# Latent attention in groups of two blocks, with four score banks and one output bank

## What is computed

```python
def mixer_mla(u, w_in, q_norm, w_uq, kv_norm, w_ukv, w_out):
    cq, ckv, k_rope, gate = jnp.split(u @ w_in, [...], axis=-1)
    q = (rmsnorm(cq, q_norm) @ w_uq).reshape(B, S, 16, 64 + 32)
    kv = (rmsnorm(ckv, kv_norm) @ w_ukv).reshape(B, S, 16, 64 + 64)
    ...
    s = (einsum('bqhd,bkhd->bhqk', q_nope, k_nope) + einsum('bqhd,bkd->bhqk', q_rope, k_rope)) * scale
    p = softmax(s, axis=-1)
    o = einsum('bhqk,bkhd->bqhd', p, v)
    return (o * silu(gate)) @ w_out
```

## Time and profile before

| | |
|---|---|
| median of 3 runs | 2837.42 us (2836.51 to 2840.32) |
| profiled execution, its own time | 2842.69 us |
| its span, mean granted clock | 2840.9 us, 0.995 |
| TensorE matmuls busy in the span | 2789.1 us (98%) |
| TensorE weight loads busy | 2323.7 us (82%) |
| VectorE, ScalarE, GpSimd busy | 1366.9, 940.3, 1237.5 us |

### The profile page before, as it was taken

One profiled execution on the slowest core, in us unless ns is written; L12 is line 12 of the kernel. 1 busy time (PEld: TensorE's weight loads), 2 busy tenths in 40 slices (PEclk: granted clock), 3 DMA queues, 4 the chain that ended last, 5 costly groups with the idle time before them and its releaser, 6 DMA issues.

```text
span 2840.9 us, 36776 instructions
## 1 busy us (share of the span) xinstructions
PE 2789.1 (98%) x13634; PEld 2323.7 (82%) x13634; DVE 1366.9 (48%) x1892; ACT 940.3 (33%) x1316; POOL 1237.5 (44%) x913
## 2 busy tenths in 40 slices
PE   7999999999999999999999999999999999999998
PEld 5888887887888888888888878888888888888886
DVE  4544566658646443046443066646442075554412
ACT  3333434763224222243222243433222231322222
POOL 2453235113554454424545533234545545354554
PEclk9999999999999999999999999999999999999999
DMA  7664234102333333332333322122333333233332
GB/s 270 181 193 129 82 94 123 36 24 67 105 95 90 96 96 96 108 105 82 96 96 104 104 83 79 59 75 89 96 96 104 104 89 97 67 114 94 100 100 95
DMA packets 106123, 284.97 MB, mean 100 GB/s; under 512 B 38669, under 2 KB 38797, under 8 KB 104675
## 3 DMA queue, kind: packets, MB, share of 16 engines
q1 hardware_dynamic: 99360, 257.64, 30.4%
q10 hardware_dynamic: 6643, 25.64, 2.7%
HBM read 280.98 MB, written 8.85 MB: 102 GB/s over the span
## 4 chain that ended last, share of the span: by engine, by line
issue 42%; PE 33%; POOL 24%; DVE 1%; DMA 0%; POOLq 0%; ACT 0%; SPq 0%
POOL w_lo L624 24%; PE ps L435 11%; PE ps L437 11%; PE ps L436 11%; DMA w_raw<-in_stream 0%; DVE x L2326 0%; DVE tmp L2320 0%; PE ps L485 0%; POOLq L622 0%; POOLq L166 0%; PE ps L513 0%; PE ps L496 0%; PE ps L480 0%; DVE u_lo L2126 0%; ACT u_hi L1557 0%
## 5 line engine op out<-in xcount | busy, mean ns | idle before, releaser
L624 POOL TENSOR_TENSOR w_lo<-w_raw,w_hi 128x512 fp32r<-128x512 f32 x904 | 1236.6, 1391 | 1590.0 <-ACT w_hi L428 1590.0
L435 PE MATMUL ps<-u_hi,w_hi 128*128 128x512 f32 x2296 | 905.3, 394 | 9.2 <-DVE u_lo L2126 5.4
L437 PE MATMUL ps<-u_hi,w_lo 128*128 128x512 f32 x2296 | 897.7, 391 | 0.0
L436 PE MATMUL ps<-u_lo,w_hi 128*128 128x512 f32 x2296 | 897.5, 391 | 0.0
L428 ACT ACTIVATE w_hi<-w_raw 128x1024 fp32r<-128x1024 f32 x452 | 475.7, 1055 | 799.2 <-PE ps L437 767.3
L435 PEld LDWEIGHTS ps<-u_hi,w_hi 128*128 128x128 f32 x2296 | 433.7, 189 | 105.6 <-DVE u_lo L2126 8.6
L437 PEld LDWEIGHTS ps<-u_hi,w_lo 128*128 128x128 f32 x2296 | 433.3, 189 | 91.2
L436 PEld LDWEIGHTS ps<-u_lo,w_hi 128*128 128x128 f32 x2296 | 433.5, 189 | 90.5 <-issue 1.9
L437 PE MATMUL ps<-h_hi,w_lo 128*128 128x512 f32 x704 | 273.9, 389 | 0.0
L435 PE MATMUL ps<-h_hi,w_hi 128*128 128x512 f32 x704 | 273.9, 389 | 0.0
L436 PE MATMUL ps<-h_lo,w_hi 128*128 128x512 f32 x704 | 273.9, 389 | 0.0
(11 more groups left out here) (307 smaller groups left out, 3089.4 us busy)
## 6 DMA issues: line engine op xcount, KB each, us to landing
w_raw<-in_stream SPq DMA_DIRECT2D x452, 512.0 KB, 3.6
late_ring<-in_ada_late ACTq DMA_DIRECT2D x32, 512.0 KB, 5.0
ada_ring<-in_ada SPq DMA_DIRECT2D x8, 1024.0 KB, 10.4
dilated_bias_rows<-dilated_bias SPq DMA_DIRECT2D x18, 244.1 KB, 5.2
band_a<-dilated_bias_rows SPq DMA_DIRECT2D x96, 28.0 KB, 2.0
x<-in_x SPq DMA_DIRECT2D x8, 256.0 KB, 8.1
bias_rows<-bias_scratch ACTq DMA_DIRECT2D x4, 512.0 KB, 7.8
out_yT<-x SPq DMA_DIRECT2D x8, 256.0 KB, 2.0
```

Source lines behind the costliest of these rows:

```text
L435: nc.tensor.matmul(o, w[0], v[0], start=start, stop=False)
L436: nc.tensor.matmul(o, w[0], v[1], start=False, stop=False)
L437: return nc.tensor.matmul(o, w[1], v[0], start=False, stop=stop)
L624: ins = nc.gpsimd.tensor_tensor(w_lo[:, s, half], w_raw[:, s, half], w_hi[:, s, half].bitcast(F32), ALU.subtract)
```

## The change

Two blocks form a group, on all three engines. TensorE issues both scores of the next group, then what there is for the next pairs, then both turns of this group, then a spread if one is due, then the values of the two blocks ahead of them. The first query product of the pair after next moves to the last group of a pair (that of pair 1 ahead of the loop), the keys to the first group and the second query product to the second group. Scores use four banks (3 to 6) in place of three (4 to 6), maxima four columns in place of two, outputs the one bank 2 in place of banks 2 and 3. TensorE now waits for all value copies before its first score, since bank 3 is one of theirs. ScalarE does both exponentials ahead of a group's two copies. VectorE does both maxima first, waits for a bank's exponential of four blocks ago in place of the last one, and takes the finished pair's steps in the four groups of the next pair; the low part of an output comes in the last group of the next pair, and at the end ahead of the last denominators.

```diff
--- before.py
+++ after.py
@@ -952,11 +952,11 @@
                 if b == 0:
                     pe.wait_ge(q_evac, Q0 + 2 * p + hh + 1)
                     pe.wait_ge(k_evac, K0 + p + 1)
-                if i >= 3:
-                    pe.wait_ge(s_read, R0 + i - 2)
+                if i >= 4:
+                    pe.wait_ge(s_read, R0 + i - 3)
                 q = [t[:, p % 2, hh, b * P:(b + 1) * P] for t in (qb_hi, qb_lo)]
                 k = [t[:, p % 2, hh, :] for t in (kb_hi, kb_lo)]
-                product(bank(4 + i % 3), q, k, True, True).then_inc(s_done, 1)
+                product(bank(3 + i % 4), q, k, True, True).then_inc(s_done, 1)
 
             def b_turn(i):
                 pe.wait_ge(s_read, R0 + i + 1)
@@ -969,12 +969,12 @@
             def b_pv(i):
                 p, b = i // 8, i % 8 // 2
                 pe.wait_ge(t_evac, T0 + i + 2)
-                if b == 0 and p >= 2:
-                    pe.wait_ge(o_evac, O0 + p - 1)
+                if b == 0 and p:
+                    pe.wait_ge(o_evac, O0 + p)
                 for k in range(QB):
                     for hh in range(2):
                         r = slice(64 * hh, 64 * hh + 64)
-                        mm = pe.matmul(ps[r, 2 + p % 2, b * P:(b + 1) * P],
+                        mm = pe.matmul(ps[r, 2, b * P:(b + 1) * P],
                                        vb[:, k, p * P + 64 * hh:p * P + 64 * hh + 64], ptb[:, (i + hh) % 3, k, :],
                                        start=k == 0, stop=k == QB - 1)
                 mm.then_inc(o_done, 2)
@@ -1005,25 +1005,28 @@
                 product(bank(j % 4), (ck_hi[:, b * P:(b + 1) * P], ck_lo[:, b * P:(b + 1) * P]),
                         (w_hi[:, slot, w], w_lo[:, slot, w]), True,
                         True).then_inc(v_turned if j < 2 * QB - 1 else chunk_used, 1)
+            pe.wait_ge(v_ready, V0 + 2 * QB)
             b_scores(0)
             b_scores(1)
-            pe.wait_ge(v_ready, V0 + 2 * QB)
-            for i in range(NB_BLOCKS):
-                p, step = i // 8, i % 8
+            b_queries(1, 0)
+            for i in range(0, NB_BLOCKS, 2):
+                p, step = i // 8, i % 8 // 2
                 if i + 2 < NB_BLOCKS:
                     b_scores(i + 2)
-                if p + 1 < NPAIR and step == 2:
-                    b_keys(p + 1)
-                b_turn(i)
-                if i and i % 2 == 0:
-                    b_pv(i - 2)
+                    b_scores(i + 3)
                 if p + 1 < NPAIR:
                     if step == 0:
-                        b_queries(p + 1, 0)
-                    if step == 4:
+                        b_keys(p + 1)
+                    elif step == 1:
                         b_queries(p + 1, 1)
-                if p and step == 6:
+                if p + 2 < NPAIR and step == 3:
+                    b_queries(p + 2, 0)
+                b_turn(i)
+                b_turn(i + 1)
+                if p and step == 2:
                     b_spread(p - 1)
+                if i:
+                    b_pv(i - 2)
             b_spread(NPAIR - 1)
             b_pv(NB_BLOCKS - 2)
 
@@ -1605,7 +1608,7 @@
                 if i >= 4:
                     act.wait_ge(t_done, T0 + i - 3)
                 at = QB * (i % 2) + i % 8 // 2
-                nc.scalar.activation(pb[:, i % 4, :], bank(4 + i % 3), ACT.Exp, bias=col[:, i % 2:i % 2 + 1],
+                nc.scalar.activation(pb[:, i % 4, :], bank(3 + i % 4), ACT.Exp, bias=col[:, i % 4:i % 4 + 1],
                                      accum_out=den[:, i // 8 % 3, at:at + 1]).then_inc(s_read, 1)
 
             chunk("b_first", 0)
@@ -1621,27 +1624,34 @@
                 nc.scalar.activation(vb[:, b, half * S:(half + 1) * S], bank(j % 4), ACT.Copy).then_inc(v_ready, 1)
             chunk("b_v", 0)
             b_exp(0)
-            for i in range(NB_BLOCKS):
-                p, step = i // 8, i % 8
-                if i + 1 < NB_BLOCKS:
-                    b_exp(i + 1)
+            b_exp(1)
+            b_query_hi(1, 0)
+
+            def b_turned(i):
                 act.wait_ge(t_done, T0 + i + 1)
                 if i >= 3:
                     act.wait_ge(o_done, T0 + 2 * ((i - 3) // 2) + 2)
                 nc.scalar.activation(ptb[:, i % 3, :, :].rearrange("p k e -> p (k e)"), bank(i % 2),
                                      ACT.Copy).then_inc(t_evac, 1)
+
+            for i in range(0, NB_BLOCKS, 2):
+                p, step = i // 8, i % 8 // 2
+                if i + 2 < NB_BLOCKS:
+                    b_exp(i + 2)
+                    b_exp(i + 3)
+                b_turned(i)
                 if p + 1 < NPAIR:
                     if step == 0:
-                        chunk("b_pair", p)
-                    if step == 1:
-                        b_query_hi(p + 1, 0)
-                    if step == 2:
                         b_keys(p + 1)
-                    if step == 5:
+                    elif step == 1:
                         b_query_hi(p + 1, 1)
-                if p >= 2 and step == 0:
-                    b_output_hi(p - 2)
-            b_output_hi(NPAIR - 2)
+                if p + 2 < NPAIR and step == 3:
+                    b_query_hi(p + 2, 0)
+                b_turned(i + 1)
+                if p + 1 < NPAIR and step == 0:
+                    chunk("b_pair", p)
+                if p and step == 3:
+                    b_output_hi(p - 1)
             b_output_hi(NPAIR - 1)
 
             norm_out(1, "b_out")
@@ -2230,7 +2240,7 @@
 
             def b_output(p):
                 dve.wait_ge(o_done, T0 + 8 * p + 8)
-                nc.vector.scalar_tensor_tensor(out=tmp[:, 2 + p % 2, :], in0=bank(2 + p % 2), scalar=0.5,
+                nc.vector.scalar_tensor_tensor(out=tmp[:, 2 + p % 2, :], in0=bank(2), scalar=0.5,
                                                in1=ggb[:, p, :], op0=ALU.mult, op1=ALU.mult).then_inc(o_evac, 1)
 
             def b_denominators(p):
@@ -2250,7 +2260,9 @@
 
             def b_max(i):
                 dve.wait_ge(s_done, R0 + i + 1)
-                nc.vector.tensor_reduce(col[:, i % 2:i % 2 + 1], bank(4 + i % 3), AX.X, ALU.max,
+                if i >= 4:
+                    dve.wait_ge(s_read, R0 + i - 3)
+                nc.vector.tensor_reduce(col[:, i % 4:i % 4 + 1], bank(3 + i % 4), AX.X, ALU.max,
                                         negate=True).then_inc(m_ready, 1)
 
             for hh in range(2):
@@ -2264,37 +2276,38 @@
                     b_key_lo(0, 0)
                     b_key_lo(0, 1)
             b_max(0)
-            for i in range(NB_BLOCKS):
-                p, step = i // 8, i % 8
+            b_max(1)
+            dve.wait_ge(grp_done, GRP0 + 3)
+            b_query_read(1, 0)
+            for i in range(0, NB_BLOCKS, 2):
+                p, step = i // 8, i % 8 // 2
                 more = p + 1 < NPAIR
-                if i + 1 < NB_BLOCKS:
-                    if i:
-                        dve.wait_ge(s_read, R0 + i)
-                    b_max(i + 1)
-                if step == 0 and p:
-                    b_denominators(p - 1)
-                if step == 1 and more:
-                    dve.wait_ge(grp_done, GRP0 + 2 * (p + 1) + 1)
-                    b_query_read(p + 1, 0)
-                elif step == 2:
+                if i + 2 < NB_BLOCKS:
+                    b_max(i + 2)
+                    b_max(i + 3)
+                if step == 0:
                     if more:
                         b_query_lo(p + 1, 0)
-                    if p >= 2:
-                        b_output_lo(p - 2)
-                elif step == 3 and more:
-                    b_key_lo(p + 1, 0)
-                    b_key_lo(p + 1, 1)
-                elif step == 4 and p:
-                    b_output(p - 1)
-                elif step == 5 and more:
-                    dve.wait_ge(chunk_used, b_chunk(p + 1) + 1)
-                    b_query_read(p + 1, 1)
-                elif step == 6 and more:
-                    b_query_lo(p + 1, 1)
-                if step == 7 and p:
-                    b_normed(p - 1)
+                        b_key_lo(p + 1, 0)
+                        b_key_lo(p + 1, 1)
+                    if p:
+                        b_denominators(p - 1)
+                elif step == 1:
+                    if p:
+                        b_output(p - 1)
+                    if more:
+                        dve.wait_ge(chunk_used, b_chunk(p + 1) + 1)
+                        b_query_read(p + 1, 1)
+                        b_query_lo(p + 1, 1)
+                elif step == 2:
+                    if p:
+                        b_normed(p - 1)
+                elif p + 2 < NPAIR:
+                    dve.wait_ge(grp_done, GRP0 + 2 * (p + 2) + 1)
+                    b_query_read(p + 2, 0)
+                if p and step == 3:
+                    b_output_lo(p - 1)
             b_denominators(NPAIR - 1)
-            b_output_lo(NPAIR - 2)
             b_output(NPAIR - 1)
             b_normed(NPAIR - 1)
```

## The result

The changed kernel takes 2852.58 us (median of 6 runs, 2848.86 to 2855.61) against 2840.34 for the kernel before (6 runs, 2836.51 to 2844.91): a ratio of 1.0043, 95% interval 1.0028 to 1.0057. Timed once more beside the kernel before it is 2851.48 against 2843.42, ratio 1.0033 (1.0021 to 1.0045). The change makes the kernel slower by 0.3 to 0.4%. The forecast was 2842.5 in a range of 2838.5 to 2847.0, and the measured time is above that range. 2.9 us of the gap are the base: the 2837.42 it was made on was a low draw of a kernel whose median over more runs is 2840.3 to 2843.4.

A forecast was written before the change was run, and what follows sets the result against it. The prediction took TensorE's own instruction stream to bound the stage, with grouping worth nothing; added waits 0.15 + 2.25 + 0.4 + 1.35 + 0.65 + 0.25 = 5.05 us on 2837.42 gave 2842.5 us, range 2838.5 to 2847.0.

The forecast's parts named there:

- walk: Step-by-step timing of a two-block group across TensorE, ScalarE and VectorE; 3.48 us per group without extras.
- (1): Pairs 0 to 6, TensorE's second query product waits for keys in bank 7: 0.15 us pair 1, 0.45 each pairs 2 to 6.
- (4): Loop end: last denominators behind pair 6's output low part delay the spread; cost 1.35 us, net 0.25.
- D: Rival, faster: a hidden drain between turn and score goes, 64 changes at 0.2 us, 12.8; 2829.7 us, chance 0.05.
- The start: First score waits for ScalarE's eighth value copy, since scores now use bank 3: 0.95 us lost, net 0.4.
- pair 0: Second query product in pair 0 waits in bank 7 for keys made late by the start: 1.35 us.
- pair 1: Second query product in pair 1 waits in bank 7 for the keys' low part: 0.15 us.
- the output bank in pair 7: Values in pair 7 wait until VectorE has read the previous pair's output from the one bank: 0.65 us.
- the second copy at 4.55: Last group of the pair before: ScalarE's second turned copy at 4.55 us, ahead of the output's high part at 5.05.
- Part (3): One output bank: values wait for VectorE's read; 0.65 us in pair 7, hidden in pairs 1 to 6, otherwise some 0.1.
- waits for pb or ptb appear: Sign in the profile after that would prove the prediction wrong; claimed absent by a microsecond's margin.
- C: Rival, slower: keys come later at bank 7 in pairs 0 to 6; with 0.5 us more, +8.5, 2846 us; chance 0.22.

The follow-up runs named there:

- the kernel with all edits: Changed kernel with fourth ptb buffer, keys' high part early, output low part late, output bank read early, last denominators first, score banks 4, 5, 6, 3; ratio 1.0003.
- the kernel with the late low part: Changed kernel with VectorE's output low part moved from the next pair's last group to behind the keys' low parts one group later; pair 18.70 us, was 19.26.

## Why the prediction was wrong

Its walk left out one wait: ScalarE's copy of a turned block waits for the values product that reads the same buffer. That is the step that failed, and it failed in two of the sum's parts, (1) and (4).

- What bounds the stage: right. TensorE's stream does, and each wait put into it is paid: taking one out gave back what it cost (0.48 us a pair, 2.3 at the end, 1.06 at the start).
- Grouping is worth nothing in the loop: right, to 0.02 us a pair. D, a hidden drain between a turn and a score, fell with the 18.27 us a pair of the kernel with all edits. The number of form changes stayed and their price too.
- The start: right (0.94 lost for 0.95), and pair 0 (1.32 for 1.35), pair 1 (0.08 for 0.15), the output bank in pair 7 (0.64 for 0.65).
- Part (1), pairs 2 to 6, is where it failed first: 0.97 us each where it had 0.45. The chain was the right one, link by link, but at one link, "the second copy at 4.55", the walk let ScalarE copy as soon as the turn was done. It left out that copy's other wait, for the values that read the third buffer. In the group before the keys this made the output's low part late on VectorE, and the first maximum moved from 1.41 to 1.94. 5 x 0.52 = 2.6 us. With a fourth buffer the pair takes 18.74 where the walk had 18.75.
- Part (4), the end: the same wait, left out again. It made the last spread 2.35 late for 1.35 and the last turns 0.50 late: 1.5 us. The fourth buffer takes both off.
- Part (3) had the wait in pair 7 right, but its 0.1 us for the other pairs, were the stall of (1) gone, is 0.32 (the kernel with the late low part). In after it is hidden, so the sum does not suffer.
- The low clock, 0.6 us in the stretch and about one behind, was in no part.
- The sign named at the end, "waits for pb or ptb appear, which the walk leaves a microsecond clear", is where it broke: ScalarE's wait for the values product, 12.5 us in 22 pieces, hits in the loop no deadline of the copies' own users, only what is queued behind them; at the end it also holds up the last turns.
- The sum: 5.05 forecast for the stage, 9.1 measured at the full clock, 9.6 with the fall. The range ended at +9.6 over a base that was itself 3 us low. Over the later medians of the kernel before the changed kernel takes 12.2 and 8.1 us more, so with the right base the second would have been inside the range; with the cause left out, that would have been luck. C, the keys later than walked, comes nearest to what happened, and I gave it 0.22. That its 0.5 us more a pair is the measured 0.52 is chance: it priced another cause (the keys' high part a copy later on ScalarE), in seven pairs and with nothing at the end.

## What to carry to other kernels

When an engine's order of work is regrouped, take every wait of every moved instruction and ask what it waits for in the new order; a buffer ring sized for the old distance (three turned blocks, values two blocks behind) becomes a wait on the engine that fills it, and all that is queued behind it moves. On a stage whose bounding engine has no idle time, the only thing grouping can win is a cost that the starts of its instructions show; here the starts showed none but the 0.4 us at the end, and the rest could only be lost.

## What the runs showed of the hardware that I had not expected

The parts of the profile that a change does not touch repeat to 0.03 us within the stage, but the part ahead of it varies by 8.4 us between profiles of the same code, and the granted clock goes with a part of that. The experiments ran on three chips, but the part varies by 5.5 us between profiles from one of them too (477.73 to 483.19). A change of a few microseconds is seen in the stage's own length in one profile (150.68 and 150.71), while the medians of the kernel before lie between 2837.42 and 2843.42.
